# Gated delta rule in a hybrid encoder block: forward and backward triangular inverses grown in one matrix per chunk

## The reference, cut to what matters

```python
dec = jnp.where(incl, jnp.exp(diff), 0.0)             # diff[i, j] = b[i] - b[j], i >= j
A = jnp.where(strict, einsum('id,jd->ij', k * beta, k) * dec, 0.0)
sol = triangular_solve(A + I, [v * beta, k * beta * exp(b)])    # u, w
attn = einsum('id,jd->ij', q, k) * dec
# scan over the chunks, S the state
v_new = u - w @ S
o = (q * exp(b)) @ S + attn @ v_new
S = S * exp(b_end) + (k * exp(b_end - b)).T @ v_new
```

## Time and profile before

| | |
|---|---|
| median of 3 runs | 2495.36 us (2493.83 to 2499.73) |
| span of the profiled execution | 2493.5 us |
| time of the profiled execution beside its span | none is given; the span stands for it |
| PE busy | 2376.0 us, 95% of the span |
| DVE / ACT / POOL busy | 1713.0 / 1015.0 / 944.2 us |
| granted TensorE clock, mean | 0.993 of 2.4 GHz |

### The profile page before, as it was taken

How to read it: one execution, slowest core, us unless ns; L and a number is a source line. 1 busy time by engine, 2 the same in 40 slices (tenths; PEclk the granted TensorE clock), 3 DMA queues, 4 the chain that set the end, 5 groups by cost and what they waited for, 6 DMA issues and landing times. The chain is left out here.

```text
span 2493.5 us, 44841 instructions
## 1 busy us (share of the span) xinstructions
PE 2376.0 (95%) x14948; PEld 1444.7 (58%) x15041; DVE 1713.0 (69%) x3600; ACT 1015.0 (41%) x1767; POOL 944.2 (38%) x612
## 2 busy tenths in 40 slices
PE   7999998989999999998999999998999999999998
PEld 6444444458878888776464565555666544444443
DVE  7435333037777777763350878898999689998887
ACT  4322423224333344333322434436999634443331
POOL 4421422413321123312432577876767422222220
PEclk9999999999999999999999999999999999999999
DMA  5321321321100011002313488887999699999994
GB/s 202 112 63 39 101 68 52 90 75 35 34 18 20 29 34 34 8 0 77 116 62 119 136 280 286 298 304 245 361 394 380 217 386 388 389 390 363 354 353 156
DMA packets 174319, 440.41 MB, mean 177 GB/s; under 512 B 17408, under 2 KB 83584, under 8 KB 174096
## 3 DMA queue, kind: packets, MB, share of 16 engines
q1 hardware_dynamic: 132752, 288.20, 33.5%
q0 software_dynamic: 36864, 134.23, 15.0%
q10 hardware_dynamic: 4608, 16.78, 1.7%
HBM read 395.11 MB, written 44.04 MB: 176 GB/s over the span
## 5 line engine op out<-in xcount | busy, mean ns | idle before, releaser
L2078 POOL TENSOR_TENSOR hid_u_lo<-hid_u,hid_u_hi 128x1024 bf16<-128x1024 f32 x128 | 290.2, 2268 | 169.2 <-ACT hid_u_hi L2062 161.4
L150 PE MATMUL bank<-hT_hi,hid_u_hi 128*128 128x384 bf16 x1024 | 335.0, 327 | 17.1 <-POOL hid_u_lo L2078 7.3
L150 PE MATMUL bank<-hT_lo,hid_u_hi 128*128 128x384 bf16 x1024 | 334.8, 327 | 0.0
L150 PE MATMUL bank<-hT_hi,hid_u_lo 128*128 128x384 bf16 x1024 | 334.8, 327 | 0.0
L214 POOL TENSOR_TENSOR w_shared_lo<-w_raw,w_shared_hi 128x1024 bf16<-128x1024 f32 x72 | 158.0, 2211 | 393.0 <-ACT w_shared_hi L209 393.0
L2062 ACT ACTIVATE hid_u_hi<-hid_u 128x1024 bf16<-128x1024 f32 x128 | 134.9, 1055 | 210.4 <-PE bank L150 150.7
L150 PE MATMUL bank<-hT_hi,w_shared_hi 128*128 128x264 bf16 (+2 forms) x699 | 200.6, 295 | 7.6 <-ACT dn_conv_in L1452 4.5
L150 PE MATMUL bank<-hT_lo,w_shared_hi 128*128 128x264 bf16 (+2 forms) x699 | 200.4, 295 | 1.4 <-ACT ex_grid L2256 1.2
L150 PE MATMUL bank<-hT_hi,w_shared_lo 128*128 128x264 bf16 (+2 forms) x699 | 200.3, 295 | 0.3
L150 PEld LDWEIGHTS bank<-hT_hi,hid_u_hi 128*128 128x128 bf16 x1024 | 100.4, 98 | 87.5 <-issue 22.1
L2769 PE MATMUL bank<-w_shared_lo,ex_gated_hi 128*128 128x512 bf16 x384 | 146.1, 380 | 5.2 <-DVE ex_gated_lo L2851 4.4
(11 more groups left out here) (513 smaller groups left out, 5818.3 us busy)
## 6 DMA issues: line engine op xcount, KB each, us to landing
hid_u<-in_peer_u SPq DMA_DIRECT2D x128, 512.0 KB
ex_v<-in_peer_v SPq DMA_DIRECT2D x128, 512.0 KB
w_raw<-in_w_ret SPq DMA_DIRECT2D x60, 512.0 KB, 4.2
expert_hidden<-hid_gelu SPq DMA_DIRECT2D x128, 192.0 KB
ex_gated<-expert_hidden SPq DMA_DIRECT2D x128, 192.0 KB
w_raw<-in_w_dn SPq DMA_DIRECT2D x32, 512.0 KB, 3.5
expert_weights<-ex_grid ACTq DMA_DIRECT2D x32, 512.0 KB
ex_weights<-expert_weights SPq DMA_DIRECT2D x64, 256.0 KB
```

The lines of the kernel that those rows point to most:

```text
L150: last = nc.tensor.matmul(out, left[l], right[r], start=start and i == 0, stop=stop and i == len(PASSES) - 1)
L2078: self.nc.gpsimd.tensor_tensor(self.us[1][:, m % 2, :, :], self.u32[:, m % RING, :, :], self.us[0][:, m % 2, :, :], ALU.subtract).then_inc ...
```

## The change

Forward and backward matrices are strictly lower and strictly upper triangular, so they fit into one matrix per chunk. The change keeps one L (`lt`), one doubled matrix (`both`) and one product of each kind for four chunks. What separates the directions at each level are masks: of the transposed copy (`right`, made by DVE out of PSUM in place of ACT's copy) and of the matrix itself (`left`, made by POOL). Parts are renamed: `turn` and `rights`, `first` (first products and `masks_in`), `second` (second products and `grow`). At the end POOL copies the two triangles of `both` into the old `xt`, and DVE writes the last blocks.

- Row broadcasts are made by transposing a column that is read with step zero along the row (`along_rows`), for the decays and for the inverse lengths, in place of products with scaled triangles and identities.
- The decay matrices become one for both directions. POOL weights it with beta (`weighted_decays`), and L, its pairs and the start of `both` come from `MATRICES` on DVE without POOL in between.
- `PROJ_K` and `PROJ_V` are cut into eight pieces each, between the parts of the levels. `SUMS` is one part after the last level, `SCALES` lies in the scan.
- The transposes to token order of k and v leave `UNIT` and stand in the first three levels (`token_v`, `token_k`, `token_m`), in bank 0.
- The taps of the convolutions are spread over the levels (q, k) and the scan (v, `SILU_2` behind the tail's squares). Bank 6 now holds the decays, the sums and Z in turn.
- POOL's order mixes `left` of levels 1 to 6 with the other work; ahead of the loop and in each head the splits of q, k, v weights come last.

```diff
@@ -1078,44 +1078,49 @@
-        early = Banks(core, [("q", 2), ("pm0", 3), ("k", 3), ("pm1", 5), ("v", 5), ("pm2", 2), ("bf", 2),
-                             ("bb", 3), ("bm", 5), ("nq", 2), ("nk", 3), ("nm", 5), ("ss", 6), ("z", 6), ("kk", 5)], DH)
-        order = [("tv", 1), ("tk", 4), ("tm", 7), ("qk", 4), ("kkm", 7)]
+        early = Banks(core, [("q", 2), ("pm0", 3), ("k", 3), ("pm1", 5), ("v", 5), ("pm2", 2), ("bf", 6),
+                             ("bb", 6), ("bm", 6), ("nq", 2), ("nk", 3), ("nm", 5), ("ss", 6), ("z", 6), ("kk", 5)], DH)
+        order = [("qk", 4), ("kkm", 7), ("tv", 0), ("tk", 0), ("tm", 0)]
...
+        pe_order = ("PROJ_Q turn0 token_v first1 PROJ_K.0 second1 PROJ_K.1 DECAYS_F turn1 token_k first2 PROJ_K.2 second2 "
+                    "PROJ_K.3 token_m turn2 PROJ_K.4 first3 PROJ_K.5 second3 PROJ_K.6 DECAYS_B turn3 PROJ_K.7 first4 PROJ_V.0 "
+                    "second4 PROJ_V.1 DECAYS_M turn4 PROJ_V.2 first5 PROJ_V.3 second5 PROJ_V.4 turn5 PROJ_V.5 first6 "
+                    "PROJ_V.6 second6 PROJ_V.7 SUMS values0 PROJ_Z0 update0 state1 values1 PROJ_Z1 update1 state2 "
+                    "values2 PROJ_Z2 update2 SCALES state3 values3 PROJ_Z3 update3 state4 PROJ_Z4 values4 PROJ_Z5 update4 "
+                    "PROJ_Z6 UNIT PROJ_Z7 tail1").split()
+        act_order = ("PROJ_Q gate_z split_z token_v EXP_F token_k SPLIT_Q token_m EXP_B PROJ_K SILU_0 SPLIT_K "
+                     "EXP_DECAY SILU_1 SPLIT_V PROJ_V scan0 LENGTHS scan1 scan2 scan3 scan4 tail0 SILU_2 tail1 tail2").split()
+        dve_order = ("TAPS GATES turn0 first1 second1 CONV_0.0 turn1 CONV_0.1 first2 ARG_F second2 CONV_0.2 turn2 CONV_0.3 "
+                     "first3 CONV_0.4 second3 turn3 ARG_B first4 ARG_M second4 CONV_1.0 turn4 CONV_1.1 first5 CONV_1.2 "
+                     "second5 CONV_1.3 turn5 CONV_1.4 first6 second6 scan0 CONV_2.0 state0 scan1 CONV_2.1 state1 scan2 "
+                     "CONV_2.2 state2 SCALES scan3 CONV_2.3 state3 scan4 UNIT tail0 CONV_2.4 tail1 MATRICES tail2").split()
...
+                def along_rows(dst, column):
+
+                    return nc.tensor.transpose(dst, column.broadcast_to([P, P]), ident[:, :])
...
+                            for c in range(NT):
+                                last = along_rows(out("b" + d)[:, c * P:(c + 1) * P], sc_next(NEGB, c, d))
...
+                            for j in range(NT):
+                                last = nc.tensor.matmul(out(f"y{d}{level}")[:, j * P:(j + 1) * P],
+                                                        lt[:, j, :], right[:, j, :],
+                                                        start=True, stop=True)
...
+                            pe.wait_ge(s["left_ready"], (LEVELS + 1) * h + level)
+                            for j in range(NT):
+                                last = nc.tensor.matmul(out(f"z{d}{level}")[:, j * P:(j + 1) * P],
+                                                        yy[:, j, :], left[:, j, :],
+                                                        start=True, stop=True)
...
+                def weighted_decays(hn, at_start):
+
+                    pool.wait_ge(s["head_next"], 2 * hn + 2)
+                    pool.wait_ge(s["dec_ready"], 2 * hn + 2)
...
+                    nc.gpsimd.tensor_tensor(db[:, :, :], dec[:, :, :], bt[:, :, :], ALU.mult)
...
+                    nc.gpsimd.tensor_tensor(dbp[:, :, :], db[:, :, :], over_chunks(masks[:, 0, 0, :]), ALU.mult)
...
+                        nc.gpsimd.tensor_tensor(left[:, :, :], both[:, :, :],
+                                                over_chunks(masks[:, 1, level, :]), ALU.mult)\
+                            .then_inc(s["left_ready"], 1)
...
+                    left_factors(1, h)
                     bk.wait_read(pool, "qk", h)
                     for i, keep in enumerate((upper, lower)):
...
+                    left_factors(2, h)
                     weights.lo(pool, h * 4 + 7, 3, 0)
+                    left_factors(3, h)
+                    left_factors(4, h)
                     if more:
-                        squares(h + 1)
+                        squares_q(h + 1)
+                    left_factors(5, h)
+                    if more:
+                        weighted_decays(h + 1, False)
+                    left_factors(6, h)
+                    for i, keep in enumerate((upper, lower)):
+                        nc.gpsimd.tensor_tensor(xt[:, i, :, :], both[:, :, :], over_chunks(keep[:, :]),
+                                                ALU.mult).then_inc(s["left_ready"], 1)
+                    if more:
+                        squares_k(h + 1)
                         for g in range(3):
                             weights.lo(pool, h * 4 + (8 + g), g, 0)
...
+                    link(nc.vector.tensor_tensor(both[:, :, :], by_chunk(out("kk")[:, :]), dbp[:, :, :], ALU.mult))
+                    nc.vector.tensor_tensor(both[:, :, :], over_chunks(ident[:, :]), both[:, :, :], ALU.subtract)\
+                        .then_inc(s["x_start"], 1)
...
+                            bk.reads(name, nc.vector.tensor_tensor(
+                                right[:, :, :], by_chunk(out(name)[:, :]),
+                                over_chunks(masks[:, 1, level + 1, :]), ALU.mult))
...
-        same = i // (2 * n) == j // (2 * n)
-        out[:, 0, level] = same & (i // n > j // n)
-        out[:, 1, level] = same & (i // n < j // n)
+        out[:, 0, level] = (i // (2 * n) == j // (2 * n)) & (i // n != j // n)
+        out[:, 1, level] = np.where(j // n % 2 == 0, j >= i, j <= i)
```

More of the change, by code:

```diff
@@ L1129, in delta_net @@
         gates = gates_of(core)
-        pe_order = ("PROJ_Q PROJ_K turn0 PROJ_V grow1 DECAYS turn1 grow2 SUMS.0 turn2 grow3 SUMS.1 turn3 grow4 SUMS.2 turn4 grow5 "
-                    "turn5 grow6 SCALES values0 PROJ_Z0 update0 state1 values1 PROJ_Z1 update1 state2 values2 PROJ_Z2 "
-                    "update2 state3 values3 PROJ_Z3 update3 state4 PROJ_Z4 values4 PROJ_Z5 update4 PROJ_Z6 UNIT "
-                    "PROJ_Z7 tail1").split()
-        act_order = ("PROJ_Q gate_z split_z PROJ_K turn0 SPLIT_Q SPLIT_K SILU_0 PROJ_V SILU_1 turn1 SPLIT_V turn2 SILU_2 EXP_B turn3 "
-                     "EXP_DECAY turn4 LENGTHS turn5 scan0 scan1 scan2 scan3 scan4 tail0 tail1 UNIT_COPY tail2").split()
-        dve_order = ("pairs TAPS GATES CONV_0 CONV_1 masks1 grow1 CONV_2.0 CONV_2.1 CONV_2.2 masks2 grow2 CONV_2.3 CONV_2.4 "
-                     "masks3 grow3 DECAY_ARG masks4 grow4 masks5 grow5 SCALES masks6 grow6 scan0 scan1 scan2 scan3 scan4 "
-                     "UNIT tail0 tail1 MATRICES tail2").split()
+        pe_order = ("PROJ_Q turn0 token_v first1 PROJ_K.0 second1 PROJ_K.1 DECAYS_F turn1 token_k first2 PROJ_K.2 second2 "
[4 rows of a table added]
+                    "PROJ_Z6 UNIT PROJ_Z7 tail1").split()
[5 more added lines that the diff above has]
+                     "CONV_2.2 state2 SCALES scan3 CONV_2.3 state3 scan4 UNIT tail0 CONV_2.4 tail1 MATRICES tail2").split()
         def run(eng, order, this, following, first_parts, ahead_in_last=()):
@@ L1204, in _, with project @@
             def _(pe):
-                def project(name, i, hn):
-                    weights.wait(pe, 4 * hn + i)
-                    early.wait_free(pe, f"pm{i}", hn)
-                    early.wait_free(pe, name, hn)
-                    for kc in range(KC):
-                        left, ends = weights.columns(0, i, kc), dict(start=kc == 0, stop=kc == KC - 1)
-                        last = pair_matmul(nc, out(name)[:, 0:HALF], left,
+                def project(name, i, hn, pieces):
+                    if pieces[0] == 0:
+                        weights.wait(pe, 4 * hn + i)
+                        early.wait_free(pe, f"pm{i}", hn)
+                        early.wait_free(pe, name, hn)
+                    for kc in pieces:
+                        columns, ends = weights.columns(0, i, kc), dict(start=kc == 0, stop=kc == KC - 1)
+                        last = pair_matmul(nc, out(name)[:, 0:HALF], columns,
                                            view(hT, slice(None), kc, slice(0, HALF)), **ends)
@@ new lines, in turned @@
+                def turned(level, h):
+                    for d, i in parts_of(level):
+                        if d == "m" and level == 3:
+                            continue
+                        if level == 0:
+                            pe.wait_ge(s["x_start"], 2 * h + (2 if d == "m" else 1))
+                        else:
+                            bk.wait_read(pe, f"z{d}{level}", h)
+                        bk.wait_free(pe, f"x{d}{level}", h)
+                        if d == "m":
+                            last = nc.tensor.transpose(out("ym1")[:, 0:P], xm[:, 1, :], ident[:, :])
+                        else:
+                            for j in range(NT):
+                                last = nc.tensor.transpose(out(f"x{d}{level}")[:, j * P:(j + 1) * P],
```

(8 more changed lines are left out.)

464 lines of the change are left out of this document (225 added, 239 removed).

## The result

The changed kernel takes 2514.49 us (median of 4 runs, 2513.45 to 2517.87) against 2495.98 for the kernel before beside it: a ratio of 1.0078, interval 1.0064 to 1.0092. It is 18.5 us slower. The forecast was 2476 with a range of 2446 to 2508, so time, range and sign all missed.

A forecast was written before the change was run, and what follows sets the result against it. TensorE, busy 95% of 2493.5 us, was taken as close to the bound, the VectorE and ScalarE chain close behind. Head period 76.1 to 71.1 nets 31, less 12 for clock falls: 19 off the median 2495.4, 2476 us (2446 to 2508).

The forecast's parts named there:

- stretch A: From the tail's end to turn0: only the Q projection stays, 5.4 us where Q and K took 11.46.
- D: Later cut, from the end of y's scalings to level 1's first product; the forecast was 8.8 us in these terms.
- stretch C: From values0 to the tail's end, scan and preparation: 26.3 us against 20.1, with TensorE waits of 2.6 and 3.1.
- stretch B: From turn0 to values0, the doubling levels with K and V projection pieces between: 39.0 us against 44.55.
- the clock: TensorE's granted clock halves after idling: one fall per head charged, 8 x 1.5 = 12 us.
- The passes that go: On TensorE, one matrix for both directions halves products and transposes: 13.8 us less per head; 15.9 with cheaper broadcasts.
- the chain of one level: In the doubling, one level alone from transposes through both products and their readers: 5.53 us.
- preparation of head 0: Ahead of the first head's levels: 4 us slower, from decays on VectorE and weighting on POOL.
- rival 2: No change, about 2495: two clock falls per head and in the last head's chain; 0.18, including 0.02 for table-change draining.
- S: Later cut, from values0 to the end of y's scalings; the forecast was 25.7 us in these terms.
- Rival 3: Slower, about 2512: POOL's left factor holds four VectorE taps right behind the second product, 36 us; chance 0.16.
- L: Later cut, from level 1's first product to values0; the forecast was 36.2 us in these terms.

The follow-up runs named there:

- e5_gates: e3_both with GATES split in two and both halves taken from ahead of VectorE's first masked copy; 2456.66 us, ratio 0.9854 to the kernel before.
- e6_short: e5_gates with tap CONV_2.4 ahead of UNIT and the 16x16 chain of MATRICES ahead of the large subtraction that releases POOL; 2447.44 us (0.9814).
- e3_both: Changed kernel with SILU_2 and its tap moved behind tail1, and PROJ_Z0 moved behind state1; 2480.12 us, ratio 0.9948 to the kernel before.
- e12_gates_only: Changed kernel with only GATES split and moved off VectorE's queue ahead of the first masked copy; 2502.12 us (1.0028).
- e7_pool: e6_short with POOL's z weight split moved ahead of its second left factor and ARG_M moved behind turn4 on VectorE; 2451.65 us (0.9849).
- e9_fill3: Changed kernel with unused 512-column products filling three TensorE waits: behind values0, ahead of tail1 and ahead of first1; 2500.66 us (1.0031).
- e10_lo: e6_short with only POOL's z weight split moved ahead of its second left factor; 2445.33 us (0.9793).
- e13_thin: e10_lo with five unused 512-column products in three small waits, ahead of second6, SUMS and update0; 2442.19 us (0.9771).
- e4_fill: Changed kernel with unused 512-column products filling two TensorE waits, behind values0 and ahead of tail1; 2508.79 us (1.0062).

## Why the prediction was wrong

The step that failed is stretch A, now called D: I added up TensorE's path there and let VectorE run 1.3 us past it, where VectorE's own queue is the longer path. Four more terms had the right mechanism and too small a size: both waits of stretch C, stretch B, and the clock.

**What held.** The passes that go, the chain of one level (5.62 a level in the changed kernel, 838.38 to 844.00, against 5.53 worked out), the broadcast-column transposes at the price of the nearest form (four in 0.60, as four ordinary ones), and the place of every wait inside the levels: 1.00 for ARG_M (0.9 forecast) and 0.46 before SUMS (0.5). The preparation of head 0 held too: turn0 starts at 578.65 where it started at 579.69 behind 5.4 us more of projection, which makes it 4.4 slower, with 4 charged. ScalarE changes its table nine times in a head of the changed kernel and four in one of before, as counted (one of them ahead of a copy, L1461 and before L1449, against the sentence above that copies need none), at 1.28 each. This is the one ahead of LENGTHS:

```profile
852.97 0.36 ACT L1524 ACTIVATE dn_v_end<-bank,dn_scal_head 128x128 f32<-128x128 f32 x1
853.35 1.28 ACT L1491 ACT_TABLE_LOAD   x1
854.64 0.26 ACT L1491 ACTIVATE dn_inverse_lengths<-wide,dn_eps 128x4 f32<-128x4 f32 x1
```

It starts 0.02 after the activation before it, and the next one follows 0.01 behind: no draining shows, so the case left for it in rival 2 is void.

**Three terms of the full-clock sum were too small**, 3.6 us per head together, 3.1 after the 0.4 for issue gaps that the forecast had on top, 22 over seven repeats:

- *Stretch A and "TAPS and GATES ... run past the copy's time by about 1.3".* This step failed in kind. It added up TensorE's path and let VectorE run 1.3 past it. VectorE's queue from y is the longer path: MATRICES 4.3, scaling and low half 2.5 (with the pause of 0.92 in it), TAPS and GATES 2.5, copy 0.68. D is 10.26, not 8.8 (+1.45). MATRICES stands there in both kernels. Before, 11.46 us of projections covered it; I moved half of them away and never asked what they had hidden. e5_gates and e6_short show it: D fell from 10.95 in e3_both to 7.84 by nothing but taking operations off that queue, and e12_gates_only shows it in the changed kernel itself, 10.26 to between 9.1 and 10.1.
- *The two waits of stretch C.* Right in place and cause, 2.98 and 4.15 instead of 2.6 and 3.1; S at full clock is 26.8, not 25.7. The second was longer because the tap that SILU_2 waits for took 1.85: it started 0.06 before the end of POOL's first q weighting and came free 0.56 after the end of the second.
- *Stretch B*, +1.1: the tap behind the z split took 2.58, which made the wait 1.56 and not 1.1, and each level took 0.09 more.

A good part of these is one thing. Beyond the 1.1 that I charged, operations of VectorE with two inputs in SBUF that met POOL cost 0.5 at the z split, 1.1 at the last tap and 1.0 at the 16x16 subtraction, about 2.6 us per head. **Rival 3 had the mechanism but not the place**: right behind the second product, where I put it, VectorE won at all four taps (CONV_0.0 took 0.48 and POOL's left factor 1.53, CONV_0.2 took 0.75 and the factor 1.80, where 1.27 is its time alone) and POOL paid. That its 2512 lies near the measured 2514.5 is chance. The Trainium skill (SBUF — State Buffer, section on the two separate sides) has issue order decide, which agrees with the 16x16 subtraction of e6_short, whose cost went when it was put ahead of the operation that releases POOL. By the same section of the Trainium skill the winner keeps the ports "for the whole instruction"; in e7_pool the loser was held through three.

**The clock.** "I charge one fall per head, 8 x 1.5 = 12." It fell about twice per head and cost some 2.7 in each repeat and 4.1 in the last head (L 35.12 against 31.62 in e9_fill3, S 20.66 against 20.06), so some 23 us and not 12. (The 1.3 us by which the first head's L is longer than the others', 3.4 us at half clock in it, come on top.) The falls at the Q projection were free, since VectorE's queue covered them; those behind PROJ_Z0 cost 2.2 to 3.3 in a head. Rival 2 had two falls per head and one in the last head's chain, and its count came out so. Of the repeats it had the reason wrong: it blamed PE's share in the thin levels, and inside those levels the clock is 1.00 (812 to 852 us). In the last head, without projections, the levels did lose clock, 12.6 us at half clock and 3.5 us of time where the rival had 7. But e6_short ran the same levels at 1.00, so thin levels alone do not settle it; what else does is open.

**The sum again**, made with what was measured: D +10.2, L +7.5, S +7.6 over seven repeats, less 2.8 for the issue allowance that these numbers already hold; clock +9.5 in the repeats; last transition +1.1; last head +3.9 (it became 5.4 longer, 1.5 was charged). That is 37 of the 38.5 us between 2476 and 2514.5. Of the remaining 1.5, 0.4 is the preparation of head 0; the rest is not assigned.

**Was the change bad?** No. With the same arithmetic and another order of parts e10_lo is 2.1% faster than the kernel before (0.9779 to 0.9806), with no unused work, and 69 us faster than the change as it was made. e13_thin has the lowest median, 2.3% under the kernel before, with products that nothing reads; that it is faster than e10_lo is not shown.

## What to carry to other kernels

Where a change takes work from the bounding engine, write down the in-order queue of each other engine between the same two events and compare lengths: what the removed work had hidden can be the new bound, and it does not show in a sum along the old path. When TensorE idles longer, its clock may fall in the next dense stretch. Here removing a wait moved that fall to the next idle place (e3_both, e4_fill), so the gain of one repair alone said little about what all of them would bring. An operation that is moved off one stretch can land on the path of another (CONV_2.4 in e6_short): look at the period, not at the stretch. And release POOL only after VectorE's small operations with two inputs in SBUF have gone, not before.

## What the runs showed of the hardware that was not expected

- A 16x16 subtraction on VectorE takes 0.16 us alone (e6_short) and 1.20 beside a POOL operation that started 0.09 earlier; a tap of 0.76 was held 3.59 us through three POOL operations that followed each other without a gap (e7_pool).
- Operations with one input in SBUF were held as well, beside POOL's weight splits: a first tap took 1.28 instead of 0.48 (changed kernel, 852.94), a copy of 128x60 took 0.87 instead of 0.21 in each of the seven repeats of e10_lo.
- The last head's levels, the same in both kernels, took 31.6 us at a mean clock of 1.00 (e6_short) and 37.3 at 0.73 (e5_gates).
- Adding unused products did not always keep the clock: with the same queue, one scan of e13_thin ran at 0.84 and the next at 1.00.
